# The order of wide and narrow matmuls inside a half weight unit, on one core

## The reference, cut to what matters

```python
proj = h @ w_in[l]                                  # first block: 2048 -> 12800 (X, Y, Q, K, V, G)
mix = sigmoid(g_rnn) * (y_rnn @ w_rnn_proj) + sigmoid(g_attn) * (y_att @ w_attn_proj)
x = x + rmsnorm(mix @ w_out[l], norm_mix_post[l])
u = square(relu(h @ w_mlp_up[l])); x = x + rmsnorm(u @ w_mlp_down[l], norm_mlp_post[l])
...
proj = rmsnorm_2(x, norm_attn) @ w_in_2             # second block: three kinds of attention
x = x + concatenate([o_a, o_b, o_c]) @ w_out_2
x = x + conv_ffn(rmsnorm_2(x, norm_mlp), w_up, conv_w, conv_b, w_down)
```

## Time and profile before

| what | value |
|---|---|
| median of three runs | 3144.35 us |
| profiled execution, its own time | 3147.61 us |
| profiled execution, its span | 3145.8 us |
| mean granted TensorE clock | 0.954 of full speed |
| TensorE (matmuls) busy | 2867.3 us, 91% |
| weight loads busy | 2476.1 us |
| VectorE, ScalarE busy | 2009.0 us, 1328.8 us |
| weights and data read | 491.63 MB on the hardware queue |

### The profile page before, as it was taken

One profiled execution on the slowest core, in us unless ns is written; L12 is line 12 of the kernel. 1 busy time (PEld: TensorE's weight loads), 2 busy tenths in 40 slices (PEclk: granted clock), 3 DMA queues, 4 the chain that ended last, 5 costly groups with the idle time before them and its releaser, 6 DMA issues.

```text
span 3145.8 us, 51627 instructions
## 1 busy us (share of the span) xinstructions
PE 2867.3 (91%) x16358; PEld 2476.1 (79%) x16358; DVE 2009.0 (64%) x3308; ACT 1328.8 (42%) x2139; POOL 158.6 (5%) x220
## 2 busy tenths in 40 slices
PE   5543989999999899999999969999989999999997
PEld 3443877777888688888888859878878888888886
DVE  6331876666666677645775473575558887588855
ACT  4223544444544444433444333444445444344443
POOL 1000020000000200000000020000011000000000
PEclk9776999999999899999999978999999999999999
DMA  4653434333455445555555533434435555555554
GB/s 131 122 117 81 169 134 166 134 134 130 164 187 187 147 149 185 200 187 184 182 183 199 187 135 134 157 111 152 125 111 187 188 187 179 195 187 187 187 171 149
DMA packets 92729, 503.26 MB, mean 160 GB/s; under 512 B 15867, under 2 KB 24347, under 8 KB 41435
## 3 DMA queue, kind: packets, MB, share of 16 engines
q1 hardware_dynamic: 84044, 491.63, 44.5%
q0 software_dynamic: 8624, 10.84, 2.8%
HBM read 491.90 MB, written 10.49 MB: 160 GB/s over the span
## 4 chain that ended last, share of the span: by engine, by line
PE 81%; DMA 8%; DVE 5%; issue 3%; ACT 2%; DVEq 1%; POOL 0%; ACTq 0%; SPq 0%; POOLq 0%
PE PS L532 46%; PE PS L536 23%; DMA w_raw<-in_w_X 4%; DMA bias_rows<-rows 1%; DVE w L1525 1%; ACT w L968 1%; PE PS L609 1%; PE PS L610 1%; PE PS L611 1%; DMA w_raw<-in_w_RG 1%; PE PS L748 1%; PE PS L547 1%; PE PS L771 1%; PE PS L695 1%; PE PS L763 1%
## 5 line engine op out<-in xcount | busy, mean ns | idle before, releaser
L1525 DVE TENSOR_TENSOR w<-w_raw,w 128x1024 fp32r<-128x1024 f32 (+3 forms) x1020 | 1105.4, 1120 | 582.8 <-ACT w L968 580.4
L968 ACT ACTIVATE w<-w_raw 128x1024 fp32r<-128x1024 f32 (+3 forms) x1020 | 945.1, 964 | 462.9 <-PE PS L536 186.0
L532 PE MATMUL PS<-h,w 128*128 128x512 f32 x3104 | 831.2, 409 | 113.1 <-ACT w L968 90.1
L532 PEld LDWEIGHTS PS<-h,w 128*128 128x128 f32 x3104 | 574.1, 194 | 263.8 <-ACT w L968 93.5
L536 PEld LDWEIGHTS PS<-h,w 128*128 128x128 f32 x3104 | 432.6, 194 | 32.1
L532 PE MATMUL PS<-u,w 128*128 128x512 f32 x1728 | 442.0, 394 | 3.7 <-ACT w L968 3.7
L536 PE MATMUL PS<-h,w 128*128 128x256 f32 x3104 | 440.2, 285 | 0.0
L532 PE MATMUL PS<-f,w 128*128 128x512 f32 x1408 | 353.1, 392 | 2.7 <-issue 2.7
L532 PEld LDWEIGHTS PS<-u,w 128*128 128x128 f32 x1728 | 308.9, 189 | 56.9 <-ACT w L968 4.1
L532 PEld LDWEIGHTS PS<-f,w 128*128 128x128 f32 x1408 | 253.3, 189 | 48.6 <-issue 2.9
L536 PEld LDWEIGHTS PS<-u,w 128*128 128x128 f32 x1728 | 241.5, 190 | 21.1
(11 more groups left out here) (262 smaller groups left out, 2685.6 us busy)
## 6 DMA issues: line engine op xcount, KB each, us to landing
w_raw<-in_w_FU SPq DMA_DIRECT2D x88, 1024.0 KB, 4.7
w_raw<-in_w_UP SPq DMA_DIRECT2D x64, 1024.0 KB, 4.7
w_raw<-in_w_DN SPq DMA_DIRECT2D x64, 1024.0 KB, 4.7
w_raw<-in_w_FD SPq DMA_DIRECT2D x64, 704.0 KB, 4.1
w_raw<-in_w_G SPq DMA_DIRECT2D x32, 1024.0 KB, 4.7
w_raw<-in_w_Q SPq DMA_DIRECT2D x18, 1024.0 KB, 4.8
w_raw<-in_w_X SPq DMA_DIRECT2D x16, 1024.0 KB, 21.8
w_raw<-in_w_Y SPq DMA_DIRECT2D x16, 1024.0 KB, 4.7
```

Of the source, the lines that this page charges most:

```text
L532: pe.matmul(PS[:, bank, :], w_hi[:, 2 * s + hf, k * P:(k + 1) * P], rhs[:, k0 + k].rearrange("p a b -> p (a b)"), start=start and k == 0, ...
L968: act.activation(w_hi[:, 2 * s + hf, 0:n * P], w_raw[:, s, off * P:(off + n) * P], ACT.Copy)\
L1525: tt(w_lo[:, slot, 0:n * P], w_raw[:, s, off * P:(off + n) * P], w_hi[:, slot, 0:n * P].bitcast(F32), ALU.subtract).then_inc(lo_ready, 1)
```

## The change

In `half_unit` the wide form loses its two loops. It now waits for lo_ready once, ahead of the first matmul, and no longer for hi_ready; then it issues for each block the matmul over 512 columns with w_hi and right behind it the matmul over 256 columns with w_lo. The form with wide=False stays as it is. The products, their number, their operands and the PSUM addresses stay the same; the order in which they are added changes.

```diff
-                if wide:
-                    pe.wait_ge(hi_ready, 2 * u + hf + 1)
-                    for k in range(n):
-                        if ready:
-                            pe.wait_ge(ready[0], ready[1] + k0 + k + 1)
-                        pe.matmul(PS[:, bank, :], w_hi[:, 2 * s + hf, k * P:(k + 1) * P],
-                                  rhs[:, k0 + k].rearrange("p a b -> p (a b)"), start=start and k == 0, stop=False)
-                    pe.wait_ge(lo_ready, 4 + 2 * u + hf + 1)
-                    for k in range(n):
-                        mm = pe.matmul(PS[:, bank, S:2 * S], w_lo[:, 2 * s + hf, k * P:(k + 1) * P],
-                                       rhs[:, k0 + k, 0, :], start=False, stop=stop and k == n - 1)
-                else:
...
+                pe.wait_ge(lo_ready, 4 + 2 * u + hf + 1)
+                for k in range(n):
+                    if ready:
+                        pe.wait_ge(ready[0], ready[1] + k0 + k + 1)
+                    w0, w1 = (w[:, 2 * s + hf, k * P:(k + 1) * P] for w in (w_hi, w_lo))
+                    r = rhs[:, k0 + k]
+                    last = stop and k == n - 1
+                    if wide:
+                        pe.matmul(PS[:, bank, :], w0, r.rearrange("p a b -> p (a b)"), start=start and k == 0, stop=False)
+                        mm = pe.matmul(PS[:, bank, S:2 * S], w1, r[:, 0, :], start=False, stop=last)
+                    else:
```

## The result

The changed kernel takes 3167.14 us (median of 4 runs, 3164.05 to 3170.11) against 3145.91 us of the kernel before (4 runs): a ratio of 1.0068, with a 95% interval of 1.0050 to 1.0086. The forecast was 3133, its range 3106 to 3160. The profiled execution took 3165.92 us with a span of 3164.1 us and a mean granted clock of 0.955; so it is 18.3 us longer than the span shown before. In the changed kernel the wide matmul is line 535, the narrow one 536, ScalarE's hi part 960, VectorE's lo part 1517, merge 1528.

A forecast was written before the change was run, and what follows sets the result against it. TensorE, busy for 2867 of 3145.8 us, was taken to bound the kernel. Cheaper pairs (-19.8 us) and the earlier wait (+8.8) sum to -11.0 from 3147.6: 3136.6, or 3133 beside the median; range 3106 to 3160.

The forecast's parts named there:

- The pair, 345 ns by choice between 341 and 353: TensorE's wide and narrow matmul together: 349 ns before, 345 interleaved, 4 ns less in each of 4960 pairs.
- The upper bound, 233 + 120 = 353: Dearest pair taken from the rows: first wide matmul of a run plus a late narrow one; 20 us lost.
- The gain that I forecast, 19.8 us: Cheaper pairs in stages where TensorE sets the pace: 4960 x 4 ns; bounds 40 us gained to 20 lost.
- The earlier wait, 8.8 us: TensorE waits for w_lo before a half's first matmul: a shift paid once a stage, 8.8 us in sum.
- the gain in UP0's first unit: After the wait for activation slices one narrow matmul is left instead of eight: 1.5 us gained.
- X's term: Stage X, six weight-transfer stalls each ending 1.26 us later for TensorE: 1 us lost, from -5 to 7.6.
- The chain of the wait in UP0: Stage UP0: TensorE starts when the lo part ends, a shift of 1.26 us once a stage, not every unit.
- the sign that the prediction gave: In UP0, idle time ahead of TensorE put down to VectorE's line 1525 instead of ScalarE's 968.
- The repeated wait in FU0: Rival: in FU0 the delay feeds back at 1.2 us for every second of 44 units, +26, about 3159; chance 0.06.
- Slower, by the weight loads: Rival: narrow matmul covers the next wide one's load too briefly, pair 233 + 120 ns, +29 us, 3173; chance 0.15.
- Clean interleave: Rival: all wide matmuls fall to 226 ns and all narrow ones to 115, -31 us, 3113; chance 0.17.
- The order changes nothing: Rival: pair stays at 348 or 349 ns, only the earlier wait is left, 3148 to 3153; chance 0.22.

The follow-up runs named there:

- halves in turn: Against the kernel before: second half of each unit waits for its lo part, then issues eight narrow and eight wide matmuls, making runs of 16; 3144.01 us, ratio 0.9992.
- the whole unit: Against the kernel before: 16 wide matmuls of a unit, then its 16 narrow ones, except units that follow activation slices, G and A2; 3142.43 us, ratio 0.9985.
- blocks of four: Against the kernel before: early wait for lo_ready, then four wide and four narrow matmuls in turn; 3166.26 us in one run.
- blocks of two: Against the kernel before: early wait for lo_ready, then two wide and two narrow matmuls in turn; 3155.98 us, ratio 1.0031.
- the early wait alone: Against the kernel before: eight wide, then eight narrow matmuls as before, but both behind one early wait for lo_ready; 3158.28 us, ratio 1.0037.
- the 384 columns: Against the kernel before: first half grouped, second interleaved, each narrow matmul widened from 256 to 384 moving columns; 3513.38 us in one run.
- the second execution: The changed kernel run once more, with no edit; 3166.72 us in one run.
- the wide one's weights: The changed kernel, but the narrow matmul takes w_hi again instead of w_lo; 3162.57 us in one run.
- an interleaved half: Against the kernel before: only the second half of each unit interleaved behind an early wait, the first half grouped as before; 3148.05 us, ratio 1.0004.

## Why the prediction was wrong

**The pair, 345 ns by choice between 341 and 353: this step failed.** The pair takes 353.3 ns in the slow rhythm, which most stages have, and 346.7 in the fast one. The upper bound, 233 + 120 = 353, was exact as a sum by luck, since its parts were not: behind a narrow matmul the wide one takes 236 on average, dearer than any late one in its run (227), and the narrow one 117, not the 113 of the first in its run. I had taken the cheapness of a first narrow matmul (here 113 to 115) for something that stands in every pair; the slow rhythm has it in one pair of three, (236, 113), (232, 118), (241, 120). The gain that I forecast, 19.8 us, became a loss of 8.7 by the medians: 28.5 us of the 34.1 between 3133 and 3167.1; the wait's term makes 3.8 and the other median of the kernel before 1.6 (3145.91 for 3144.35). That the order would pay the full +4.2 ns in all 4960 pairs, 21 us, didn't happen either: C2 and FD1 were fast, Q (left out of the table) was fast in most halves and 0.5 us shorter, G, where TensorE works on other things between the halves and 15 of the 64 halves were fast, grew by only 1.57 us for its 512 pairs, and in MA, O, UP0 and UP1 the slow pair (16 x 353.3 = 5.65 us a unit) left the splitting (5.68) hardly slower than TensorE, so that wait and order were not both paid there. (The 5.62 us a unit that the prediction read off for the splitting is one of two values in turn, 5.62 and 5.74; the reading did not enter the sum.) Why the wide matmul takes 236 between two narrow ones stays open.

**The earlier wait, 8.8 us (10.3 without the gain in UP0's first unit): mechanism right, one effect missed.** Alone it costs 12.6 us by the medians. Named one by one: UP0 1.29 and UP1 1.26 (1.3 each); MA and O 1.23 (1.6); FU0 1.19 ahead of its first matmul and 0.72 at its third unit (2.2 for both); FD0 and FD1 1.97 (2.0); C2 and B2 1.12 (0.9); Y's 1.54 is not carried on, V starts only 0.3 us later by it. These are 8.8 us where the prediction had 9.3. What I had missed is the clock in FU0, 1.2 us: the earlier wait lengthens TensorE's pause, and the unit behind it ran at 0.77 of full speed instead of 1.00. The column has another 2.7 us in VC, OA and OB. For these the early wait is not shown as the cause: VC was also 1.6 us longer with halves in turn and 3.2 with the whole unit and with blocks of four, its second part waiting for other work between. X's term, 1 us from -5 to 7.6, can't be told from its spread: G began anywhere from 6.4 us earlier (halves in turn) to 0.2 later (blocks of two) than before. The gain in the first unit of UP0 was 0.65 us, not 1.5.

**The chain of the wait in UP0.** It goes as foretold, once a stage and not in every unit. With the early wait alone each unit from the third on starts 0.05 to 0.23 us behind the end of its lo part, and yet the whole stage grew by 1.29 us. In the changed kernel the list of waits names line 1517 once, for 0.2 us; the sign that the prediction gave, idle time put down to that line, is missing from the later units, since the slow pair had brought TensorE behind the splitting. The repeated wait in FU0 did not appear (2.06 us inside the stage, not 26).

**The rivals.** "Slower, by the weight loads" came nearest: its price of 353 is the slow rhythm's, its time of 3173 is 6 us above the result, since part of the stages ran fast or had the wait in common with it. Its reason, the load's short cover, is not borne out by the 384 columns. "Clean interleave" is out by far. "The order changes nothing" would have been within 0.7 ns of the blocks of two, but not of the change made. The back-to-back rule of the Trainium skill (TensorE: Matmul & The Clock Gate, "Back-to-back issue gap"), an estimated 325 ns a pair, is not met by any order that ran: the lowest is 346.7. The page gives that formula for an isolated matmul.

**What stays open:** what decides between the two rhythms. It isn't the granted clock (1.00 in both), the weights' place, or the program alone, since two executions of one kernel differ. It is mostly kept through a stage, in DN1 over the 496 pairs behind its first unit, and it can be chosen anew where one distance is longer, as at DN1's 17th pair. FU1 changed from fast to slow without such a distance, at the same pair, the third of its eleventh unit, in the second execution and with the wide one's weights. Uniform widths are not free of rhythms either: in VC, where all matmuls have 256 columns, the distances settle at 120 ns each before, but go 120, 120, 125, 117, 118 in turn in part of the changed kernel's profile. There the mean stays 120, so that only the two widths in turn are seen to have two prices.

## What to carry to other kernels

Before reordering matmuls that follow one another without a gap, take the distance from start to start at each place of a run, and don't extend the price of a first matmul to a sequence that the trace doesn't show: bound it, and give both bounds their due, since here the dear bound was the true one. Fewer changes of width were safe here, one in every pair was not: one change back and forth per 16 blocks gave 347.9 ns, one per 8 gave 349.2, and one per block 346.7 or 353.3, not fixed by the program and mostly the dear one. And an operand that is fetched late but used late should be waited for late: asking for w_lo eight matmuls earlier cost 12.6 us without any work added, 1.2 of it because a longer pause of TensorE was followed by a lower granted clock.

## What the runs showed that I had not expected

- Two locked rhythms of one instruction stream: (236, 113), (232, 118), (241, 120) ns, 353.3 a pair, and about (230, 117), 346.7 a pair. One stage of 512 pairs is 181.0 or 177.5 us long by it, and in DN1 the one turned into the other behind a single distance that was 50 ns longer.
- A run of wide matmuls behind a run of narrow ones starts with 233, 236, 228, 232, 231 ns before it settles at 227; behind an interleaved half it takes 236 and is at 227 from the second on.
- Half as many or twice as many changes do not order the price: 348.3 for blocks of two, 350.8 for four, 349.2 for eight.
- The opening of A2 ran at a granted clock of 0.78 in one profile and 1.00 in another, 4.3 us of difference that the pair has no part in. A comparison of two single profiles has such terms in it; here the order costs 5.9 us by the profiles and 8.7 by the medians.
